# Cache pages turned in 32x32 blocks by DVE, from pages loaded with every fourth token on a quarter of the partitions

## The reference

```python
ch = kp.reshape(B, nc, CMP_STRIDE, KH, HD).transpose(0, 1, 3, 2, 4).reshape(B, nc, KH, CMP_STRIDE * HD)
half = CMP_STRIDE * HD
ha = ch @ w1[:half]
hb = ch @ w1[half:]
h = ha[:, :-1] + hb[:, 1:] + pe.reshape(-1) @ w1
return jax.nn.silu(h) @ w2
```

## Time and profile before

| | |
|---|---|
| median of three runs | 2832.79 us (2829.26 to 2835.66) |
| profiled execution | 2827.5 us |
| its span, first to last instruction | 2825.6 us |
| PE busy in the span | 2591.2 us, 92% |
| DVE, ACT busy | 1217.6 us (43%), 678.4 us (24%) |
| HBM read, written | 262.07 MB, 18.17 MB |
| page loads of the stage | 512 of 192 KB, 3.5 us from issue to landing (median) |

### The profile page before, as it was taken

One profiled execution on the slowest core, in us unless ns is written; L12 is line 12 of the kernel. 1 busy time (PEld: TensorE's weight loads), 2 busy tenths in 40 slices (PEclk: granted clock), 3 DMA queues, 4 the chain that ended last, 5 costly groups with the idle time before them and its releaser, 6 DMA issues. The chain is left out here.

```text
span 2825.6 us, 39688 instructions
## 1 busy us (share of the span) xinstructions
PE 2591.2 (92%) x13852; PEld 2072.5 (73%) x13852; DVE 1217.6 (43%) x2869; ACT 678.4 (24%) x1639; POOL 286.5 (10%) x310
## 2 busy tenths in 40 slices
PE   8988999869889899999989889997897998999997
PEld 6866777557687688888778667775665976888886
DVE  2833555455456744201047245555454576440012
ACT  1023444323422211100011234443234222110001
POOL 0500000000040211001014000000001311110010
PEclk9996999879999999999999989998899999999998
DMA  6214655234401042432042155552342112223310
GB/s 187 68 52 167 192 178 179 87 94 136 120 17 54 16 119 75 127 82 60 1 117 75 23 187 170 181 186 71 109 134 80 40 32 75 76 74 90 82 38 32
DMA packets 335273, 273.91 MB, mean 97 GB/s; under 512 B 52897, under 2 KB 330850, under 8 KB 334874
## 3 DMA queue, kind: packets, MB, share of 16 engines
q1 hardware_dynamic: 308680, 253.65, 30.1%
q10 hardware_dynamic: 26450, 18.35, 2.3%
HBM read 262.07 MB, written 18.17 MB: 99 GB/s over the span
## 5 line engine op out<-in xcount | busy, mean ns | idle before, releaser
L2659 PE MATMUL psum<-ff,HT 128*128 128x272 f32 x1536 | 353.3, 392 | 0.0
L447 PE MATMUL psum<-xT,ring 128*128 128x272 f32 x1408 | 326.7, 395 | 22.0 <-PEq L169 22.0
L2659 PEld LDWEIGHTS psum<-ff,HT 128*128 128x128 f32 x1536 | 291.8, 190 | 60.2
L447 PEld LDWEIGHTS psum<-xT,ring 128*128 128x128 f32 x1408 | 269.4, 192 | 78.3 <-issue 22.5
L1051 PE MATMUL psum<-chunks,W 128*128 128x512 f32 x512 | 242.0, 634 | 10.6 <-DVE chunks L1173 10.6
L1173 DVE COPY chunks<-psum 64x256 f32<-64x256 f32 x512 | 215.2, 420 | 28.5 <-PE psum L1030 21.2
L2505 PE MATMUL psum<-yT,HT 128*128 128x272 f32 x896 | 216.4, 399 | 0.0
L1030 PE MATMUL psum<-cst,ring 128*128 128x128 f32 x1536 | 192.5, 277 | 19.1 <-DMA ring<-in_cache_nsa_kv 19.1
L1051 PEld LDWEIGHTS psum<-chunks,W 128*128 128x128 f32 x512 | 102.6, 203 | 138.3 <-issue 138.3
L2505 PEld LDWEIGHTS psum<-yT,HT 128*128 128x128 f32 x896 | 173.2, 194 | 36.5
L1030 PEld LDWEIGHTS psum<-cst,ring 128*128 128x128 f32 x1536 | 177.0, 147 | 28.4 <-DMA ring<-in_cache_nsa_kv 21.0
(11 more groups left out here) (526 smaller groups left out, 3527.0 us busy)
## 6 DMA issues: line engine op xcount, KB each, us to landing
ring<-in_cache_nsa_kv SPq DMA_DIRECT2D x512, 192.0 KB, 3.5
ring<-in_w_up SPq DMA_DIRECT2D x32, 1024.0 KB, 5.6
ring<-in_cache_nsa_kv SPq DMA_DIRECT2D x384, 64.0 KB, 1.9
HT<-in_w_down SPq DMA_DIRECT2D x12, 2048.0 KB, 9.0
ring<-in_w_in SPq DMA_DIRECT2D x20, 1024.0 KB, 5.2
ring<-in_cache_nsa_kv ACTq DMA_DIRECT2D x128, 64.0 KB, 2.2
HT<-in_w_out SPq DMA_DIRECT2D x8, 1024.0 KB, 5.1
yT<-in_w_down SPq DMA_DIRECT2D x4, 2048.0 KB, 12.4
```

Source lines behind the costliest of these rows:

```text
L447: last = pe.matmul(psum[0:w.shape[1], 2 * (t % 3) + h, 0:HALF], w, S.xT[:, k, h * HALF:(h + 1) * HALF], start=(k == 0), stop=(k == KT - 1))
L2659: last = pe.matmul(out[h], down[t % 3][:, k, :], f[:, k, x], start=(k == 0), stop=(k == FT - 1))
```

## The change

**Pages.** The load writes the source as `(a i) n -> i a n` with i = 4: partition 32 i + a of the slot takes token 4 a + i. Bytes and row length are the same; the source pattern has dimensions 4 x 32 x 384, the destination 128 x 384 (128 x 1 x 384 in the instruction).

**Turning.** DVE turns a whole group with one instruction, in 32x32 blocks, from the ring straight into `turned` in SBUF. After it, partition 32 i + d holds feature d (of 32) of token residue i: four tokens of 32 features on the 128 partitions, and a feature's half f chooses the column block. PE's turnings, the copies into `chunks` and `kt`, and those two tiles go.

**First layer.** `W1`'s rows are loaded in the order that matches: 32 transfers of 32x4x64 in place of 4 of 128x8x64. `hidden` runs after each pair of groups, 2 x 8 products of 128 columns, in place of 2 x 8 of 512 after the eighth group.

**Scores.** The turned keys are the fixed operand, four products a group (2 heads x 2 feature halves). The queries are spread into `q_wide`, where residue i has its own 8 columns and zeros elsewhere, so that the 32 columns of a product are residue x query. The scores' order of tokens changes with it, and the softmax's addition of the block bias reads PSUM in the order that undoes it.

**Around it.** ACT takes over the copies behind the second layer and the window. The query stage becomes part of the stage of the scores. For the prompt POOL makes 32 copies of 32x128 in place of 8 of 64x256, and the position vector rides as two more columns of the prompt's product in place of a product of its own (`pe_n` is loaded in 4 pieces).

```diff
 def compression_loads(S, l, sp, s):
-    sp.dma_start(S.pe_n[:, :], layer(io.cmp_pe, l).rearrange("c (h j t) d -> (c h j) (t d)", h=2, j=8)).then_inc(s.cmp, 16)
+    for c in range(2):
+        for f in range(2):
+            src = layer(io.cmp_pe, l)[c].rearrange("(h t i) (f d) -> f (h t) i d", h=2, t=4, f=2)[f]
...
-            src = layer(io.cmp_w1, l)[c, 1024 * h:1024 * h + 1024].rearrange("(j q) e -> q j e", q=P)
-            sp.dma_start(S.W1[:, c, :, HD * h:HD * h + HD], src).then_inc(s.cmp, 16)
+            for i in range(4):
+                src = layer(io.cmp_w1, l)[c, 1024 * h:1024 * h + 1024].rearrange("(t i f d) e -> i f d t e", t=4, i=4, f=2)
+                for f in range(2):
+                    sp.dma_start(S.W1[32 * i:32 * i + 32, c, f::2, HD * h:HD * h + HD], src[i, f]).then_inc(s.cmp, 16)
 def natural_keys(S, l, ctx):
...
-                    for i in range(2):
-                        pool.tensor_copy(tok[HD * i:HD * i + HD, c, k, :],
-                                         H(T_KV + c)[HD * k:HD * k + HD, i:SEQ:2]).then_inc(s.paired, 1)
+                    for f in range(2):
+                        for i in range(4):
+                            pool.tensor_copy(tok[32 * i:32 * i + 32, c, f, k * P:k * P + P],
+                                             H(T_KV + c)[HD * k + 32 * f:HD * k + 32 * f + 32, i:SEQ:4]).then_inc(s.paired, 1)
...
-            pe.wait_ge(s.paired, 8)
-            for c in range(2):
-                for j in range(8):
-                    last = pe.matmul(psum[:, 4 + c, 0:64], S.W1[:, c, j, :], tok[:, c, :, j::8], start=(j == 0), stop=(j == 7))
+                pe.wait_ge(s.paired, 16 * c + 16)
+                for j in range(8):
+                    last = pe.matmul(psum[:, 4 + c, 0:66], S.W1[:, c, j, :], tok[:, c, j % 2, j // 2::4], start=(j == 0), stop=(j == 7))
 def sample_scores(S, l, ctx):
...
-                            sp.dma_start(cache[:, g % slots, j, :], src[:, 0:3 * P]).then_inc(loaded[g % slots], 16)
+                            sp.dma_start(cache[:, g % slots, j, :], src[:, 0:3 * P].rearrange("(a i) n -> i a n", i=4)).then_inc(loaded[g % slots], 16)
...
-                    for c in (2, 0, 1):
-                        for j in range(gp):
-                            last = pe.transpose(psum[:, 3 * (g % 2) + c, j * P:j * P + P],
-                                                cache[:, g % slots, j, c * P:c * P + P], C["ident"])
...
+                    x = turned[:, (g // 2) % 2, 2, :, :, (g % 2) * P:(g % 2) * P + P]
+                    out = psum[:, 2, g * 64:g * 64 + 64].rearrange("p (i k r) -> p i k r", i=4, k=KVH)
+                    for k in range(KVH):
+                        for f in range(2):
+                            last = pe.matmul(out[:, :, k, :], x[:, k, f, :], q_wide[:, ds(b, 1), k, f, :].rearrange("p a (i r) -> p (a i) r", i=4),
+                                             start=(f == 0), stop=(f == 1))
...
+                def hidden(b, n, first):
                     for c in (1, 0):
...
+                        out = psum[:, c, :].rearrange("p (k n) -> p k n", k=KVH)[:, :, 64 * n:64 * n + 64]
                         for j in range(8):
-                            last = pe.matmul(psum[:, hidden_bank[c], :], S.W1[:, c, j, :], chunks[:, c, :, j, :],
+                            last = pe.matmul(out, S.W1[:, c, j, :], turned[:, n % 2, c, :, j % 2, j // 2::4],
                                              start=(j == 0), stop=(j == 7))
...
+                def turn(b, g, first):
+                    dve.wait_ge(loaded[g % slots], b * (16 * gp * NG // slots) + 16 * gp * (g // slots + 1))
+                    if not first or g >= 4:
+                        dve.wait_ge(s.used, b * (2 * NPAIR) + 2 * (g // 2 - 1))
+                    dst = turned[:, (g // 2) % 2, :, :, :, (g % 2) * P:(g % 2) * P + P]
+                    dve.transpose(dst.rearrange("p c k f (j a) -> p (c k f) j a", a=32),
+                                  cache[:, g % slots, :, :].rearrange("p j (f d) -> p f j d", d=32)).then_inc(s.turned, 1)
...
 def sample_softmax(S, l, ctx):
...
-                dve.tensor_tensor(p_sel[:, 512 * q:512 * q + 512].rearrange("p (j n) -> p j n", n=64),
-                                  psum[:, q % 4, :].rearrange("p (j n) -> p j n", n=64), bc(block_bias[:, 8 * q:8 * q + 8], 64),
-                                  ALU.add).then_inc(s.added, 1)
+                dve.tensor_tensor(p_sel[:, 512 * q:512 * q + 512].rearrange("p (j a i) -> p j a i", a=16, i=4),
+                                  psum[:, q % 4, :].rearrange("p (i j a) -> p j a i", a=16, i=4),
+                                  bc(bc(block_bias[:, 8 * q:8 * q + 8], 16), 4), ALU.add).then_inc(s.added, 1)
```

More of the change, by code:

```diff
@@ L950, in sample_scores @@
     H = lambda t: S.HT[:, t - 6, :]
[L951 to L960, removed]
     with ExitStack() as c:
@@ L1034, in score @@
                 def score(b, g, first):
+                    pe.wait_ge(s.turned, b * NG + (g + 1))
                     if not first and g == 0:
                         pe.wait_ge(s.sc_copied, b)
[L1037 to L1041, removed]
@@ L1111, in _, with compressed @@
             def _(act):
-                def vc_out(b):
+                def compressed(b):
+                    for n, c in enumerate((1, 0)):
+                        act.wait_ge(s.added, b * 4 + (2 * n + 2))
+                        act.activation(hid[:, c, :], hid[:, c, :], ACT.Silu, bias=S.pe_h[:, c:c + 1]).then_inc(s.swish, 1)
                     act.wait_ge(s.second, b + 1)
-                    act.wait_ge(s.kc_copied, b + 1)
+                    act.copy(kc[:, :], psum[:, 5, 0:NCB]).then_inc(s.kc_copied, 1)
                     for j in range(2):
@@ L1117, in vc_out @@
                         act.copy(S.vc[0:m, j, ds(b, 1), :].rearrange("p a n -> p (a n)"),
[L1118 to L1135 removed]
+                                 psum[0:m, 6, j * P:j * P + P]).then_inc(s.vc_copied, 1)
@@ new lines, in compressed @@
+                    act.wait_ge(s.cmp_scored, b + 1)
+                    for j in range(2):
+                        m = P - j
+                        act.copy(S.st_cmp[0:m, j, cols(b)], psum[0:m, 7, j * 16:j * 16 + 16]).then_inc(s.cmp_copied, 1)
+                def sequence(b, before):
+                    if before is not None:
+                        compressed(before)
+                    act.wait_ge(s.w_turned, b + 1)
+                    act.copy(wkt, psum[:, 3, :]).then_inc(s.w_copied, 1)
+                    act.wait_ge(s.scored, b + 1)
+                    act.copy(S.st_sel[:, :, cols(b)], psum[:, 2, :].rearrange("p (t r) -> p t r", r=16)).then_inc(s.sc_copied, 1)
+                    act.wait_ge(s.w_scored, b + 1)
+                    act.copy(S.st_win[:, :, cols(b)], psum[:, 4, 0:64].rearrange("p (t r) -> p t r", r=16)).then_inc(s.w_sc_copied, 1)
@@ L1144, in _ @@
+                act.wait_ge(s.placed, KVH * GRP)
+                for i in (1, 3):
+                    for f in range(2):
+                        spread(act.copy, i, f, s.q_act)
                 sequence(0, None)
@@ L1187, in sequence, with add_halves @@
+                def add_halves(b, first):
+                    if not first:
+                        dve.wait_ge(s.second, b)
                     for n, c in enumerate((1, 0)):
@@ L1189, in sequence @@
                         for k in range(KVH):
-                            dve.tensor_tensor(hid[HD * k:HD * k + HD, c, :], psum[0:HD, hidden_bank[c], k * NCH:k * NCH + NCB],
+                            dve.tensor_tensor(hid[HD * k:HD * k + HD, c, :], psum[0:HD, c, k * NCH:k * NCH + NCB],
                                               hb[:, c, k, :], ALU.add).then_inc(s.added, 1)
-                sequence(0, None)
-                with dve.Fori(0, NB - 1) as i:
-                    sequence(i + 1, i)
-                kc_out(NB - 1)
-                cmp_out(NB - 1)
+                def sequence(b, before, second):
+                    first = before is None
+                    for g in range(NG):
+                        if g == 2 and not first:
+                            add_halves(before, second)
+                        turn(b, g, first)
+                dve.memset(S.q_rows[:, :], 0.0).then_inc(s.zero, 1)
+                dve.memset(q_wide[:, :, :, :, :], 0.0).then_inc(s.zero, 1)
+                dve.wait_ge(s.zero, 2)
+                rows = S.q_rows[:, :].rearrange("p (b k g t) -> p b k g t", b=NB, k=KVH, g=GRP)
+                for k in range(KVH):
+                    r = slice(64 * k, 64 * k + 64)
+                    for g in range(GRP):
+                        dve.tensor_copy(rows[r, :, k, g, :], H(T_Q + g)[r, SEQ:].rearrange("p (b t) -> p b t", b=NB)).then_inc(s.placed, 1)
+                dve.wait_ge(s.placed, KVH * GRP)
+                for i in (0, 2):
+                    for f in range(2):
+                        spread(dve.tensor_copy, i, f, s.q_dve)
+                sequence(0, None, False)
```

(4 more changed lines are left out.)

161 lines of the change are left out of this document (48 added, 113 removed).

## The result

The changed kernel takes 3324.03 us (median of 4 runs, 3323.44 to 3325.61) against 2834.22 for the kernel before it on the same chip: a ratio of 1.173 (95% interval 1.170 to 1.175), slower by about 490 us. The forecast was 3366, in a range of 3255 to 3515.

A forecast was written before the change was run, and what follows sets the result against it. PE bound the old kernel (92% busy); page loads on 4 engines would bind the new. Stages at 576.7 us a layer add 536: 2827.5 + 536 - 3 = 3360, plus 5 to the runs' median, 3366 us; range 3255 to 3515.

The forecast's parts named there:

- The engines of a page: Page load: source's outermost dimension of 4 was taken to give 4 DMA engines a page, where before there were 16.
- the landing of 8 us or more: Sign in the profile page: a page's median time to landing would rise from 3.5 us to 8 or more.
- The price of a page: Page load on 4 engines: 2.15 us a page, between 1.95 and 2.41, giving 69.6 us a sequence against 36.16.
- What lies beside it: Other work of a sequence, hidden under 69.6 us: PE 27 (54 at 1.2 GHz), DVE turning 13.6, SP 19 to 27.
- The first rival: Page load: destination's 128 rows keep 16 engines, 0.60 us a page, PE binds at 27 us; 2693 us, chance 0.12.
- the side "faster": Whole kernel: chance 0.12 that the change makes it faster, the case of sixteen engines with a fast turning.
- The start and the tail: Scores stage of each layer: 2.3 us before the first page's transfer, 17.6 us from the last page to the next stage.
- Small terms: Prompt keys, SP's weight transfers and the softmax's additions, over both layers: together -3 us.
- layer 0 SP waits for the bias table behind them anyway: SP's 31 more weight transfers, 10 to 19 us of issue: taken as 0, at worst +5 us.
- POOL's copies: Prompt's keys: 32 quarter copies at 0.3 us each, gaining about 2 us a layer; between -3 (0.2) and +3 (0.46).
- The softmax's read of PSUM with a step: Softmax's 16 additions of 512 elements, reading PSUM with a stride: 0, at most doubled, which is +9 us.

The follow-up runs named there:

- the counts 2, 8 and 16: Changed kernel's page source in 2, 8 or 16 groups instead of 4, the last two with runs of 8 columns: 4361.38, 2804.24 and 2694.06 us.
- the kernel of 16 groups: Changed kernel with page source in 16 groups of 8 rows, hidden layer reading runs of 8 columns, weights and softmax order following: 2694.06 us.

## Why the prediction was right

**The engines of a page** (step: an outermost dimension of 4 gives 4 engines). Right, and shown: 4 small packets a page, the loss follows the pattern into the kernel before and goes with it, and the counts 2, 8 and 16 follow. The other signs that the forecast named came too (100 GB/s, a DMA share of 0.28, sequences 66 us apart, DVE and PE waiting for pages), but for the landing of 8 us or more: the profile gives no landing time for these pages.

**The price of a page** (step: 2.15 us, between 1.95 and 2.41). 2.03, so 65.9 us a sequence for 69.6. The mean rate of the filling, 20.4 GB/s an engine, was taken while 16 engines drew together; four alone run at 24, near the best slice of the earlier trace rows, and leaning to the middle made the error. The stages took 552.0 and 550.8 us for 576.7 each: 50.6 us under the sum.

**What lies beside it.** DVE's turning was forecast at 1.7 us and took 1.78. SP and ACT stayed hidden. PE was hidden too, but its term was mis-sized: "15.7 us" for the hidden layer, from the turning and the score, which read neighbouring columns. The change reads with a step of 16 B, and that is 128 x 0.232 = 29.7 us at the full clock, 39 to 40 us a sequence in place of 27. It cost nothing under 66 us of loads. The nearest row with a step, 32 records in 7.07 us, could not have shown it. Its granted clock, the column before the last two, was 0.50:

```profile
243.46:250.53 7.07, 7.07 (x33) 6.88 (x33) 0.83 (x5) 0.21 (x1) 0.00 (x0) 0.50 0.23 80
```

At that level a record without a step takes as long: 0.235 us a turning against 0.22 here. So no row that I read had the price of a step at the full clock, and the forecast took a row without a step for it and didn't say so.

**The first rival** (16 engines still, 2693 us) fell as a forecast of this kernel, and its working was wrong as well: with 16 engines and the change's own reads the time is 2879 us, slower than before. That 2694 was measured belongs to a kernel with both cures. So with the right price of a step the side "faster" had hardly a case left, and the 0.12 on it was too much.

**The start and the tail** (step: 2.3 and 17.6 us). The tail took 19.7, from the last turning at 792.83 to the next stage at 812.50. That leaves 4 to 5 us of the stage's 552.0 for the start. Both were too short, by some 4 us a layer together.

**Small terms** (step: -3). They came to +12.5, what the span grew by, 498.2, less the two stages' 245.5 and 240.1. Layer 0's stage opens 6.4 us later than before (260.54 for 254.09). The timeline shows two causes, in brackets the idle time before each row:

```profile
200.22 15.43 SPq L835 DMA_DIRECT2D W<-in_cmp_w  x32
...
218.29 8.45 SPq L779 DMA_DIRECT2D line_dram<-ring  x4
...
221.20 0.69 DVE L689 COPY ring<-psum 128x512 f32<-128x512 f32 x1 [7.09 <-DMA line_dram<-ring]
...
221.94 3.78 PE L724 MATMUL psum<-ring 33*128 33x512 f32 x4 [3.44 <-DVE ring L689]
...
238.06 14.56 POOL L864 COPY tok<-HT 32x128 f32<-32x128 f32 x32 [42.49 <-POOLq L169]
...
252.67 3.68 PE L884 MATMUL psum<-tok,W 128*128 128x66 f32 x16 [5.05 <-POOL tok L864]
```

SP's 32 weight transfers stand ahead of the bias lines' stores, so DVE waits for a buffer of those lines, and PE 3.4 us for DVE. The step was "layer 0 SP waits for the bias table behind them anyway": it does, but the table's makers wait for SP too. POOL's copies took 14.56 / 32 = 0.455 us each, the upper bound of the forecast (0.3 was taken), and PE waited 5.05 us for the second half. From POOL's first copy to the stage of the scores it is 22.5 us in place of 19.6 in layer 0 (234.51 to 254.09 before) and 22.6 in place of 18.8 in layer 1, 6.7 us together. The first copy itself comes 3.6 us later than before in layer 0, of which 1.4 were there when the stage of convolution and pooling began, ahead of SP's weight loads. So the two causes make up about 9 of the 12.5 us; for the rest no run shows a cause.

The softmax's read of PSUM with a step cost nothing: its 16 additions took 10.4 us, and 10.5 in the kernel before.

The sum closes: -50.6 for the stages and +15.5 for the small terms is -35, and the span grew by 498.2 us where 533 were forecast.

## What to carry to other kernels

Read a rearranged load's outermost dimension before its bytes: here the source's 4 capped the engines, although the destination had 128, and the layout that the turning needs was to be had with 16 groups as well, by dealing the tokens out differently. Price a term at the access pattern that it will have, not at the nearest instruction of the same shape: a product that was cheap on neighbouring columns took twice the time with a step of 16 B. And a cost that is hidden must still be sized right, since the next repair uncovers it: with the load alone cured, the time was 2879 us, still above the 2832 of the kernel before.

## What the runs showed of the hardware

One record of a float32 product of 128 columns took 3.74 / 32 = 0.117 us on runs of 8 columns and no more with a step of 8 B (2692.86 us the kernel, against 2694.06), but 0.232 us with a step of 16 B, at a granted clock of 1.00 in both of the windows above, and 7.63 / 32 = 0.238 with the clock at 0.50 for most of the stretch, where the runs of 8 took 6.41 / 32 = 0.200. (The Trainium skill, Advanced Engine Details and Errata, "Memory Cachelines", says of SBUF that two hits in a line of 16 bytes are needed for full speed. Both steps agree with that: 8 B gives two float32 to a line, 16 B one. The page gives no price; here it is a factor of 2.)

POOL's quarter copies took 0.455 us when each column came from a step of 16 B, and 11.06 / 32 = 0.346 us in the kernel of 16 groups, which reads runs of four; this row is of that kernel:

```profile
237.25 11.06 POOL L866 COPY tok<-HT 32x128 f32<-32x128 f32 x32 [41.94 <-POOLq L169]
```
